# One program block for both stages, an early load of the first block's indices, and the first weight split ahead of the block table

## The reference

```
xn = rmsnorm(x);  a, u, v, ga, gb = split(xn @ w_in)
h  = x + (sigmoid(ga) * (pool_mixer(a) @ w_up_pool) + sigmoid(gb) * (gmlp_mixer(u, v) @ w_up_gmlp)) @ w_out
hn = rmsnorm(h)                                  # the expert stage's input
g  = argmax(hn @ w_group + b_group)              # one of 4 groups of experts
e1, e2 = the two best of the group's 4 experts by hn @ w_router + b_router
y  = h + sum over e in (e1, e2) of weight_e * (silu(hn @ w_gate[e]) * (hn @ w_up[e])) @ w_down[e]
out = rmsnorm(y)
```

## Time and profile before

| | |
|---|---|
| device time, median of 3 runs | 1948.63 us (1948.27 to 1950.48) |
| the profiled execution, its own time | 1948.81 us |
| its span (first to last instruction) | 1946.7 us |
| mean granted TensorE clock | 0.973 |
| PE busy | 1849.3 us, 95% of the span |
| VectorE busy | 1052.7 us, 54% |
| ScalarE busy | 726.1 us, 37% |
| GpSimd busy | 445.8 us, 23% |

### The profile page before, as it was taken

The page is one execution under the profiler, slowest core; times in us unless marked ns, Lnnn a source line. Parts: engine busy times, 40 slices in busy tenths (PEclk is TensorE's granted clock), DMA queues, the critical chain, the costliest instruction groups (busy, mean ns, idle before and its releaser), DMA issues. The chain is left out here.

```text
span 1946.7 us, 26924 instructions
## 1 busy us (share of the span) xinstructions
PE 1849.3 (95%) x9272; PEld 1551.7 (80%) x9273; DVE 1052.7 (54%) x1995; ACT 726.1 (37%) x1356; POOL 445.8 (23%) x623
## 2 busy tenths in 40 slices
PE   7899999999999999999999972999999999999995
PEld 5899987788888788888788862888888887888884
DVE  5634343455454645444645335577677766666572
ACT  4332232333333333333333222444454444444441
POOL 2000000000200000100001004445444545454453
PEclk9899999999999999999999985999999999999998
DMA  7223233423234423235222524588678867766642
GB/s 230 88 69 105 88 112 113 154 86 106 90 130 139 143 87 94 80 130 173 85 89 87 197 106 141 183 286 303 221 265 308 299 207 260 245 216 212 211 158 75
DMA packets 167146, 310.02 MB, mean 159 GB/s; under 512 B 19024, under 2 KB 85584, under 8 KB 167066
## 3 DMA queue, kind: packets, MB, share of 16 engines
q1 hardware_dynamic: 133706, 223.61, 34.0%
q0 software_dynamic: 33360, 85.33, 12.4%
HBM read 256.66 MB, written 85.27 MB: 176 GB/s over the span
## 5 line engine op out<-in xcount | busy, mean ns | idle before, releaser
L64 PE MATMUL bank<-xT_hi,wh 128*128 128x512 f32 (+1 forms) x960 | 340.2, 354 | 7.4 <-ACT S L764 5.4
L65 PE MATMUL bank<-xT_lo,wh 128*128 128x512 f32 (+1 forms) x960 | 339.7, 354 | 0.0
L66 PE MATMUL bank<-xT_hi,wl 128*128 128x512 f32 (+1 forms) x960 | 338.6, 353 | 0.0
L812 DVE TENSOR_TENSOR wl<-raw,wh 128x512 fp32r<-128x512 f32 x352 | 219.3, 684 | 201.7 <-ACT wh L602 201.6
L1824 PE MATMUL bank<-gu_hi,ex_hi 128*128 128x512 f32 x640 | 254.5, 398 | 8.4 <-DVE ex_lo L1709 6.0
L1826 PE MATMUL bank<-gu_hi,ex_lo 128*128 128x512 f32 x640 | 250.6, 391 | 0.0
L1825 PE MATMUL bank<-gu_lo,ex_hi 128*128 128x512 f32 x640 | 250.0, 391 | 0.0
L602 ACT ACTIVATE wh<-raw 128x512 fp32r<-128x512 f32 x352 | 192.1, 619 | 85.0 <-PE bank L1246 54.7
L546 POOL TENSOR_TENSOR rs<-ms,half_neg 128x1 f32<-128x1 f32 (+1 forms) x51 | 33.9, 665 | 805.2 <-DVE ms L850 805.2
L64 PEld LDWEIGHTS bank<-xT_hi,wh 128*128 128x128 f32 x960 | 181.8, 189 | 36.0 <-issue 9.8
L66 PEld LDWEIGHTS bank<-xT_hi,wl 128*128 128x128 f32 x960 | 182.1, 190 | 25.3
(11 more groups left out here) (243 smaller groups left out, 3243.8 us busy)
## 6 DMA issues: line engine op xcount, KB each, us to landing
raw<-in_w_in SPq DMA_DIRECT2D x56, 1024.0 KB, 5.1
raw_gate_up<-in_w_gate SPq DMA_DIRECT2D x16, 2048.0 KB, 8.2
raw_gate_up<-in_w_up SPq DMA_DIRECT2D x16, 2048.0 KB, 12.1
raw_d<-in_w_down SPq DMA_DIRECT2D x16, 2048.0 KB, 8.6
raw<-in_w_out SPq DMA_DIRECT2D x16, 1024.0 KB, 6.5
raw<-in_w_up_pool SPq DMA_DIRECT2D x16, 512.0 KB, 3.5
raw<-in_w_up_gmlp SPq DMA_DIRECT2D x16, 512.0 KB, 4.6
h<-in_x_prompt SPq DMA_DIRECT2D x16, 512.0 KB, 4.9
```

What stands on the lines that cost most here:

```text
L64: nc.tensor.matmul(out, lh, rh, start=(i == 0), stop=False)
L65: nc.tensor.matmul(out, lh, rl, start=False, stop=False)
L66: last = nc.tensor.matmul(out, ll, rh, start=False, stop=(i == n - 1))
L812: lo = lambda out, x, hi: tt(out, x, hi.bitcast(F32), ALU.subtract)
```

## The change

Both stages now stand in one program block: each engine runs its list of the token stage and goes on with its list of the expert stage. What the barrier stood for is done by waits on single semaphores (`h_out`, `hn_out`, `lg_full`, `o_full`, `scattered`, `tab_ok`). Tiles of the expert stage lie where tiles of the token stage lay, as before.

- POOL's 13 fills move into the token stage, after the last GpSimd power of the norm of h and before the last group's scatters (`begin_gpsimd`).
- After its wait for the scatters, POOL loads only the first block's indices (column 0 of the slots, 128 pieces of 12 bytes) straight into `idx`, gathers the first rows with them, and only then issues the load of all slots; it waits for that, and for `tab_ok`, ahead of the loops.
- ScalarE and TensorE no longer wait for `tab_ok` ahead of the first block, but behind it. VectorE writes the table (`table()`) between the split of expert 0's weights and the low half of the first rows. The start values that unlock the split are now written to a tile of their own (`begun`) ahead of it.
- The history is one tile, transposed by four transposes in place of eight into one PSUM bank; VectorE copies it behind the first low rows, and SP stores it behind the load of expert 0's down weights and ahead of expert 1's loads.
- SP loads g_final as soon as the last output projection is done (`o_full`), not behind the barrier.

The core of the diff, without lines that are only indented anew (lines that are left out are marked):

```diff
-        phase_one(nc, shared)
-        phase_three(nc, shared)
+        shared.update(phase_one(nc, shared))
+        shared.update(phase_three(nc, shared))
+        with nc.Block() as block:
+            @block.sync
+            def _(sp):
+                shared["on_sync"](sp)
+                shared["experts_on_sync"](sp)
...
+            @block.tensor
+            def _(pe):
+                shared["on_tensor"](pe)
+                shared["experts_on_tensor"](pe)
...
-        hist = [sb("hist_prompt", [P, 4, 16]), sb("hist_sample", [P, 4, 16])]
+        hist_both = sb("hist", [P, 4, 32])
+        hist = [hist_both[:, :, 0:16], hist_both[:, :, 16:32]]
-        histT = xb[0:16, 0:2, 0:HALF]
+        histT = gmix[0:32, 0:HALF]
...
-            for c, out in ((0, v["new_pool_prompt"]), (1, v["new_pool_sample"])):
-                sp.wait_ge(hist_ok, c + 1)
-                sp.dma_start(out[0, 0, :, :], histT[1:16, c, :]).then_inc(hist_out, 16)
-            sp.wait_ge(hist_out, 32)
...
                 if not ph.next:
+                    v["begin_gpsimd"]()
                     scatter(ph)
...
-            for c in range(2):
-                dve.wait_ge(hist_full, c + 1)
-                nc.vector.tensor_copy(histT[:, c, :], (bankA[0], bankA[1])[c][0:16, :]).then_inc(hist_ok, 1)
...
-            for c in range(2):
-                pe.wait_ge(a_free[c], FILLED[c])
-                for m in range(4):
-                    last = nc.tensor.transpose((bankA[0], bankA[1])[c][0:16, m * P:(m + 1) * P], hist[c][:, m, :],
-                                               ident[:, :])
-                last.then_inc(hist_full, 1)
-        block_stack.close()
+            for m in range(4):
+                last = nc.tensor.transpose(psum[2][0:32, m * P:(m + 1) * P], hist_both[:, m, :], ident[:, :])
+            last.then_inc(hist_full, 1)
...
         def on_sync(sp):
...
+            sp.wait_ge(v["o_full"], 2 * NT)
             sp.dma_start(v["gf"][:, :], v["g_final"].rearrange("(a n) -> a n", a=1).broadcast_to([P, D]))\
                 .then_inc(v["gf_in"], 16)
             sp.wait_ge(x_rows_in, 16)
             sp.dma_start(raw_d[:, :, :], v["w_down"][0, 0].rearrange("(k p) f -> p k f", p=P)).then_inc(down_in, 16)
+            sp.wait_ge(v["hist_ok"], 1)
+            for row, out in ((1, v["new_pool_prompt"]), (17, v["new_pool_sample"])):
+                sp.dma_start(out[0, 0, :, :], v["histT"][row:row + HIST, :]).then_inc(v["hist_out"], 16)
             with sp.Fori(1, NG) as a:
                 load(a * EPG, a)
...
+            sp.wait_ge(v["hist_out"], 32)
...
+        def begin_gpsimd():
-                pool.dma_start(slots[:, :, :], slot_dram.rearrange("(p n) o -> p n o", p=P)).then_inc(slots_in, 16)
             nc.gpsimd.memset(spare[:, :], 0.0).then_inc(spare_ok, 1)
...
             nc.gpsimd.memset(sg[:, :], 0.0).then_inc(spare_ok, 1)
+        def on_gpsimd(pool):
+            with nc.allow_non_contiguous_dma(reason="the first block's indices"):
+                pool.dma_start(idx[:, :], slot_dram.rearrange("(p n) o -> p n o", p=P)[:, 0, :]).then_inc(idx_in, 16)
             pool.wait_ge(spare_ok, 13)
-                pool.wait_ge(slots_in, 16)
-                pool.wait_ge(tab_ok, 1)
+            pool.wait_ge(v["h_out"], 16 * NT)
+            for s in range(3):
+                pool.wait_ge(v["hn_out"][s], 16 * v["stores_of_hn"](NPROMPT, s))
...
-                rows_of_x(slice(0, 1), 0)
+            wait_apart(pool, idx_in, 16, passed_pool)
+            rows_of_x()
+            pool.dma_start(slots[:, :, :], slot_dram.rearrange("(p n) o -> p n o", p=P)).then_inc(slots_in, 16)
             rows_of_h()
             rows_of_z()
+            pool.wait_ge(slots_in, 16)
...
+            pool.wait_ge(tab_ok, 1)
             experts(pool, lambda e, lo: None, per_block, skip_first=True)
...
         def on_scalar(act):
             act.wait_ge(spare_ok, 13)
-                act.wait_ge(tab_ok, 1)
+            act.wait_ge(v["h_out"], 16 * NT)
...
             per_block(0, 0, 0, 0, True)
+            act.wait_ge(tab_ok, 1)
             experts(act, split, per_block, peel=True, skip_first=True)
...
         def on_vector(dve):
...
+            def table():
                 ts(blk_i[:, :].rearrange("p (b a) -> p b a", b=EPG), running[:, :].rearrange("p (a b) -> p b a", b=EPG),
                    float(P - 1), None, ALU.add)
...
-                nc.vector.memset(sums[0][:, 1:2], 0.0).then_inc(gu_done, 1)
-                nc.vector.memset(sums[0][:, 2:3], 0.0).then_inc(final_ok, 1)
+            nc.vector.memset(begun[:, 0:1], 0.0).then_inc(gu_done, 1)
+            nc.vector.memset(begun[:, 1:2], 0.0).then_inc(final_ok, 1)
+            dve.wait_ge(v["h_out"], 16 * NT)
+            for s in range(3):
+                dve.wait_ge(v["hn_out"][s], 16 * v["stores_of_hn"](NPROMPT, s))
+            dve.wait_ge(v["lg_full"], NT)
...
             split(0, 0, begin=True)
+            table()
             rows_low(1)
+            dve.wait_ge(v["hist_full"], 1)
+            copy(v["histT"], psum[2][0:32, :]).then_inc(v["hist_ok"], 1)
+            dve.wait_ge(v["gf_in"], 16)
             add(1, 1)
             per_block(0, 0, 0, 0, True)
...
         def on_tensor(pe):
-                pe.wait_ge(tab_ok, 1)
             rows_of_x(16)
...
             per_block(0, 0, 0, 0, first=True, begin=True)
+            pe.wait_ge(tab_ok, 1)
             experts(pe, lambda e, lo: None, per_block, peel=True, skip_first=True)
```

More of the change, by code:

```diff
@@ L1755, in mean @@
-                def mean(n):
-                    dve.wait_ge(z_ss, n)
-                    ts(msz[:, :], ssz[:, :], 1.0 / D, EPS, ALU.mult, ALU.add).then_inc(z_ms, 1)
-                def scale(n):
-                    dve.wait_ge(z_rs, n)
-                    dve.wait_ge(moved_y, n)
-                    stt(final[:, :], z[:, :], rsz[:, 0:1], v["gf"][:, :], ALU.mult, ALU.mult).then_inc(final_ok, 1)
-                def split(i, lo, begin=False):
-                    dve.wait_ge(gate_in, 16 * i + 16)
-                    dve.wait_ge(gu_done, lo + 1)
-                    copy(gu[0][:, 0, :], raw_gu[:, 0, :])
-                    dve.drain()
-                    for k in range(2 * KD):
-                        if k == KD + 4 and not begin:
-                            add(lo + 1, lo + 1)
-                        if k:
-                            dve.wait_ge(e_hi, SPLITS_ACT * i + k)
-                        lo_half(gu[1][:, k, :], raw_gu[:, k, :], gu[0][:, k, :]).then_inc(e_lo, 1)
@@ L1797, in _ @@
-                split(0, 0, begin=True)
-                rows_low(1)
-                add(1, 1)
-                per_block(0, 0, 0, 0, True)
-                experts(dve, split, per_block, peel=True, skip_first=True)
-                total = dve.value_load(blk_tab[0:1, 2 * NE - 1:2 * NE], min_val=1, max_val=MAXBLK)
-                hidden_low(total - 1)
-                for n in (total + 1, total + 2):
-                    add(n, total + 1)
-                    mean(n)
-                    scale(n)
@@ new lines, in add, with mean @@
+            def add(n, stored):
+                dve.wait_ge(y_done, n)
+                dve.wait_ge(final_ok, n)
+                dve.wait_ge(z_out, 16 * stored)
+                dve.wait_ge(h_rows_in, 16 * n)
+                for c in range(2):
+                    cols = slice(c * HALF, (c + 1) * HALF)
+                    stt(z[:, cols], bankY[c][:, :], idx_h[:, 1:2].bitcast(F32), h_rows[:, cols],
+                        ALU.mult, ALU.add).then_inc(z_ok, 1)
+            def mean(n):
+                dve.wait_ge(z_ss, n)
+                ts(msz[:, :], ssz[:, :], 1.0 / D, EPS, ALU.mult, ALU.add).then_inc(z_ms, 1)
@@ new lines, in scale, with split @@
+            def scale(n):
+                dve.wait_ge(z_rs, n)
+                dve.wait_ge(moved_y, n)
+                stt(final[:, :], z[:, :], rsz[:, 0:1], v["gf"][:, :], ALU.mult, ALU.mult).then_inc(final_ok, 1)
+            def split(i, lo, begin=False):
+                dve.wait_ge(gate_in, 16 * i + 16)
+                dve.wait_ge(gu_done, lo + 1)
+                copy(gu[0][:, 0, :], raw_gu[:, 0, :])
+                dve.drain()
+                for k in range(2 * KD):
+                    if k == KD + 4 and not begin:
+                        add(lo + 1, lo + 1)
+                    if k:
+                        dve.wait_ge(e_hi, SPLITS_ACT * i + k)
+                    lo_half(gu[1][:, k, :], raw_gu[:, k, :], gu[0][:, k, :]).then_inc(e_lo, 1)
@@ new lines, in on_vector @@
+            split(0, 0, begin=True)
+            table()
+            rows_low(1)
+            dve.wait_ge(v["hist_full"], 1)
+            copy(v["histT"], psum[2][0:32, :]).then_inc(v["hist_ok"], 1)
+            dve.wait_ge(v["gf_in"], 16)
+            add(1, 1)
+            per_block(0, 0, 0, 0, True)
+            experts(dve, split, per_block, peel=True, skip_first=True)
```

(2 more changed lines are left out.)

522 lines of the change are left out of this document (261 added, 261 removed).

## The result

The changed kernel took 1936.84 us (median of four executions, 1935.61 to 1938.67) against 1948.86 us for four executions of the kernel before on the same chip: ratio 0.9936, 95% interval 0.9922 to 0.9950, 12.0 us less (12.5 by the ratio). Run once more beside other kernels, it took 1938.92 us against 1948.22: ratio 0.9951 (0.9938 to 0.9964), 9.3 us less. The forecast was 9.0 us less, 1939.8 us.

A forecast was written before the change was run, and what follows sets the result against it. TensorE's 30.98 us idle at the experts' start, behind barrier, table and split, was taken as the bound; scatters, index load, gather and transposes put the first product at 1198.5, not 1207.52: 1948.81 - 9.0 = 1939.8 us, range 1936.7 to 1944.7.

The forecast's parts named there:

- The low end of the range, 1936.7: Whole kernel: scatters not held, gather landing in 4.1 us and index load in 1.5 us.
- term (1): POOL's last eight scatters: seven start inside the split and lose 0.3 us each, 2.1 us; POOL passes at 1187.1.
- the rest as before, shifted: Profile outside the forecast stretch: expected unchanged except for moving earlier.
- The rival with no hold: Scatters beside VectorE's split: they lose nothing, gain 11.1 us, 1937.7 us; chance 0.17.
- (2), (3): POOL's index load lands in 2.1 us; gather starts 0.86 us after the semaphore, transposes 4.53 us after that.
- the slow small load of the rival with the other sign: POOL's index load lands as slowly as start-up loads, 16.0 us: slower, 1953.7 us; chance 0.03.
- (4): TensorE's first block: transposes take 1.94 us, the product follows 2.0 us after their end, at 1198.5.
- The clock: TensorE at the experts' start: low clock costs the same as before; otherwise 1.2 us less gain.
- Table and split covered: VectorE and ScalarE: split ends about 1185.5, table by 1190, both before the rows; cost nothing.
- The norm beside the fills: Last rows' norm on VectorE: rival has POOL's fills hold it 2.2 us, gain 6.8, 1942.0 us; chance 0.07.
- The second block's gather and the first addition in time: Behind the first product: gather has 12 us against a longest landing of 8.0; h and z come before needed; cost nothing.
- The fills' new place: POOL's 13 fills ahead of the scatters: run in POOL's wait, end the table's hold under cover; cost nothing.

The follow-up runs named there:

- early rows: Changed kernel with the first block's indices loaded and rows gathered ahead of the last group's scatters, unproven full block assumed; 1927.19 us, 0.9890 of the kernel before.
- the table first: Changed kernel with VectorE writing the table ahead of the weight split; 1938.42 us, 0.9952 of the kernel before.
- 84 dummy products: Changed kernel plus 84 unread TensorE products between the history's transposes and the first rows; 1940.46 us, 0.9960 of the kernel before.
- barrier kept: Changed kernel with two program blocks and the barrier between them again; 1942.63 us, 0.9967 of the kernel before.
- split after: Changed kernel with VectorE's table at once and its split only after all scatters have landed; 1939.24 us, 0.9956 of the kernel before.
- early rows first: First rows gathered ahead of the last scatters, their high and low halves ahead of the splits, against the changed kernel; 1932.82 us, 0.9919 of the kernel before.
- The warm kernels: Changed kernel plus 84 or 100 unread TensorE products ahead of the first rows; 1940.46 and 1937.20 us, 0.9960 and 0.9949 of the kernel before.
- one block only: Changed kernel with all slots loaded first, fills behind the scatters and table ahead of the split again; 1942.34 us, 0.9967 of the kernel before.
- 100 products: Changed kernel plus 100 unread TensorE products between the history's transposes and the first rows; 1937.20 us, 0.9949 of the kernel before.
- all slots first: Changed kernel with the first block's indices copied from the load of all slots again; 1941.67 us, 0.9966 of the kernel before.

## Where the prediction failed, and what it had right

The path was the one forecast: the barrier goes, the split and the table are covered, the gather's chain binds, and what is won at the first product is won at the end. What failed is the size. The sum gave 9.0 us; the stretch it was summed for gained 10.2 to 10.3 in the two profiles of the changed kernel, and the two comparisons of times gave 12.0 and 9.3. The low end of the range, 1936.7, stands for a gain of 12.1, so the first comparison (12.0, or 12.5 by the ratio) lies at that end or beyond it, where only every term at its most favourable would have brought it.

Two steps account for that. The first is term (1), the hold of the scatters, forecast at 2.1 us and measured at 0.6. The second is that the prediction put everything outside the stretch at nothing ("the rest as before, shifted") and added its range up from the terms of the chain alone. The token stage and the tail were together 2.1 us shorter in the first pair of profiles, and they differ by 4.0 and 3.4 us between two executions of the changed kernel. The 1.7 us from 10.3 to 12.0 is thus no part of the mechanism as far as the profiles show, and that the second comparison came near 9.0 is luck as well.

**(1) Scatters, the step that was mis-sized.** 2.1 us of hold were forecast, from the mean of fourteen indirect DMAs of the expert stage; it was 0.6: in both profiles of the changed kernel one scatter of the eight was held by 0.5 us. POOL's next load started 1.42 us after the last scatter's end, 0.3 more than the 1.1 of the earlier trace rows, so that this term was 1.2 us too long in all, nearly the whole of the 1.3 that the sum missed. The fourteen DMAs are gathers and stores of whole rows, and none of them is a scatter of 12 bytes. But scatters were no better guide. The trace of before has four that start well inside the token stage's subtractions `wl` on VectorE; the prediction used only the one at 504.65. The others, at 515.04, 775.04 and 1045.34, are

```profile
515.04 1.18 POOL L556 DMA_INDIRECT slot_table<-pay,dest  x1 [0.30 <-issue]
775.04 1.42 POOL L556 DMA_INDIRECT slot_table<-pay,dest  x1 [0.30 <-issue]
1045.34 1.11 POOL L556 DMA_INDIRECT slot_table<-pay,dest  x1 [0.30 <-issue]
```

and the four take 0.6 us more than 0.96 on the mean, which for seven scatters would have been 4.1 us. No group of rows of before gives a hold of 0.6 us for all eight.

The rival with no hold (gain 11.1) was off by 0.8 on the other side. The rule of the Trainium skill weighed there ("SBUF — State Buffer", "Who interferes with whom") has tensor_tensor not stall a DMA's descriptors and gives that rival's sum, a little nearer than mine. The traces agree with it for most scatters and not for all, and the measurement decides: beside the same back-to-back subtractions of VectorE one scatter was held in the changed kernel, four or five with early rows, none with the table first or with 84 dummy products, each time by 0.5 us; and none where no split ran beside them (the eight of before, of barrier kept and of split after). ScalarE's half of the split isn't the holder: with early rows first it was over at 1185.09, and the scatters at 1185.56 and 1187.37 still took 1.50 and 1.51. What decides which scatters are held stays open.

**(2), (3) Small load and gather.** From the load's issue to the gather's start 2.96 us measured, 2.96 forecast (2.1 and 0.86); from there to the transposes 4.41 against 4.53. Both as forecast, and the slow small load of the rival with the other sign did not occur.

**(4) Rows to product.** 3.97 us from the transposes' start to the product against 3.94.

**The clock.** About the same cost as before, as assumed: the pitch went from 0.43 to 0.23 us 3.6 us after the first product (4.4 in the repeat, and 4.4 in the kernel before by the same reading). The warm kernels took at most 1.3 us of it away.

**Costed at nothing.** Table and split covered: right. The norm beside the fills: not held (1.29 against 1.28), that rival falls. The second block's gather and the first addition in time: right. The fills' new place: I named only the hold of the table's first operation, which goes; that ScalarE's split waits for the fills I had passed over, and with the fills in their old place that wait, together with the table's order, costs 1.0 us (one block only).

## What to carry to other kernels

A barrier between two stages costs more than its drain: it also forbids the work of the next stage that needs nothing from the last, and here the two together were 7.7 us of 10.3 (4.0 and 3.7). When a chain is freed, write down for each engine what its list begins with (a wait for fills is enough to undo an early start), and measure from the last common instruction to the first product, since the rest of a kernel can vary by several us (4.0 and 3.4 here between two executions of one kernel). A range for the whole time has to hold that variation too, and not only the terms of the chain. A first product that comes sooner pays only until the second block's data binds: with early rows first, 11.5 us sooner at the first product were 2.6 us later two blocks on.

## What the runs showed of the hardware

- A scatter of 12-byte rows by POOL beside VectorE's subtractions of two SBUF tiles was held by 0.5 us (1.5 instead of 0.96) or not at all in the changed kernel and its variants; which of them is held was not the same in kernels whose split ran beside the same scatters. In the kernel before, four such scatters took 1.11 to 2.48 us, and fourteen gathers and stores of rows beside splits 1.28 us on the mean.
- TensorE's granted clock fell from 1.00 to 0.50 in idle stretches of 3.7 us (84 products) and of 2.0 us, or just behind it (100 products). A stretch of dummy work that ends with a short wait ahead of the real work gave 1.3 us at most.
- The gather of 128 rows landed 4.4 to 4.7 us after its start with no load of weights and no split beside it, and 8.0 to 8.4 us when the loads of the next expert's weights had begun 3 to 4 us ahead of it; a load of 408 KB of slots took 3.5 us with no load of g_final ahead of it (all slots first), against 4.7 in the kernel before.
- At the end of a program block, POOL's next DMA stood 5.37 us behind its last scatter in two kernels, against 1.42 without the block's end.
